# Two of four late modulation products moved from VectorE to GpSimd, their loads from ScalarE's queue to SyncE's

## What is computed

```
def _layer(x, c, positions, norm_g, w_ada, b_ada, w_in, ...):
    mod = jax.nn.silu(c) @ w_ada + b_ada
    shift, scale, gate = jnp.split(mod, 3, axis=-1)
    h = _rmsnorm(x, norm_g) * (1.0 + scale[:, None, :]) + shift[:, None, :]
    proj = h @ w_in
    ...
    xbc = jax.nn.silu(_causal_dwconv(xbc, conv_w, conv_b))
    ...
    y = _ssd(xs, dt, A, Bm, Cm) + d_skip[:, None] * xs      # uses cumulated sums of dt * A
    ...
    out = mixed @ w_out
    return x + gate[:, None, :] * out
```

## Time and profile before

| | |
|---|---|
| median of three executions | 3406.31 us |
| the profiled execution, its own time | 3412.05 us |
| its span in the trace | 3410.0 us |
| mean granted TensorE clock | 0.984 |
| PE busy | 3296.2 us, 97% |
| DVE busy | 1748.1 us, 51% |
| ACT busy | 1191.9 us, 35% |
| POOL busy | 410.4 us, 12% |

### The profile page before, as it was taken

How to read it: one execution, slowest core, us unless ns; L and a number is a source line. 1 busy time by engine, 2 the same in 40 slices (tenths; PEclk the granted TensorE clock), 3 DMA queues, 4 the chain that set the end, 5 groups by cost and what they waited for, 6 DMA issues and landing times.

```text
span 3410.0 us, 44406 instructions
## 1 busy us (share of the span) xinstructions
PE 3296.2 (97%) x18526; PEld 2620.8 (77%) x18526; DVE 1748.1 (51%) x2533; ACT 1191.9 (35%) x1884; POOL 410.4 (12%) x318
## 2 busy tenths in 40 slices
PE   6999999899999999999999999999999999999999
PEld 5776777686677888887777778888888887678887
DVE  6854455644446743336767654433565334454333
ACT  3334442434443432224333342222343224332221
POOL 0000010000001311002222211100101011011110
PEclk9899999899999999999989999999999999899999
DMA  5631122221122333224200013322323323012332
GB/s 218 201 124 56 56 99 83 78 87 62 56 77 73 105 105 99 97 88 128 69 20 3 19 46 121 99 94 89 103 86 99 97 89 93 10 64 94 99 98 81
DMA packets 83911, 295.47 MB, mean 87 GB/s; under 512 B 9472, under 2 KB 12800, under 8 KB 81664
## 3 DMA queue, kind: packets, MB, share of 16 engines
q1 hardware_dynamic: 78384, 270.61, 24.5%
q10 hardware_dynamic: 5328, 22.02, 2.0%
HBM read 283.94 MB, written 8.65 MB: 86 GB/s over the span
## 4 chain that ended last, share of the span: by engine, by line
PE 83%; DVE 7%; ACT 2%; issue 2%; POOL 1%; DMA 1%; DVEq 0%; ACTq 0%; POOLq 0%
PE acc L478 66%; PE acc L1508 1%; DVE w_lo L389 1%; DMA late_ada<-in_ada 1%; PE acc L2487 1%; PE acc L3261 1%; PE aux L3225 1%; PE aux L1789 1%; ACT w_hi L382 1%; PE acc L1820 1%; DVE ssd_ex L1410 1%; PE acc L2491 1%; PE acc L2477 1%; PE aux L2444 1%; PE aux L3230 1%
## 5 line engine op out<-in xcount | busy, mean ns | idle before, releaser
L478 PE MATMUL acc<-op_hi,w_hi 128*128 128x512 f32 x2624 | 1086.6, 414 | 25.7 <-ACT conv_sums L1201 11.8
L478 PE MATMUL acc<-op_hi,w_lo 128*128 128x512 f32 x2624 | 1030.5, 393 | 0.0
L478 PE MATMUL acc<-op_lo,w_hi 128*128 128x512 f32 x2624 | 1029.3, 392 | 0.0
L382 ACT ACTIVATE w_hi<-raw 128x1024 fp32r<-128x1024 f32 (+2 forms) x476 | 494.4, 1039 | 1529.4 <-PE acc L478 1499.5
L389 DVE TENSOR_TENSOR w_lo<-raw,w_hi 128x1024 fp32r<-128x1024 f32 (+2 forms) x476 | 577.0, 1212 | 291.9 <-ACT w_hi L382 291.6
L478 PEld LDWEIGHTS acc<-op_hi,w_hi 128*128 128x128 f32 x2624 | 496.5, 189 | 186.0 <-issue 83.9
L478 PEld LDWEIGHTS acc<-op_hi,w_lo 128*128 128x128 f32 x2624 | 495.9, 189 | 107.5
L478 PEld LDWEIGHTS acc<-op_lo,w_hi 128*128 128x128 f32 x2624 | 497.6, 190 | 102.9 <-issue 10.1
L478 PE MATMUL acc<-ffn_hi,w_hi 128*128 128x512 f32 x800 | 311.5, 389 | 0.0
L478 PE MATMUL acc<-ffn_hi,w_lo 128*128 128x512 f32 x800 | 311.3, 389 | 0.0
L478 PE MATMUL acc<-ffn_lo,w_hi 128*128 128x512 f32 x800 | 311.3, 389 | 0.0
(11 more groups left out here) (583 smaller groups left out, 3889.3 us busy)
## 6 DMA issues: line engine op xcount, KB each, us to landing
raw<-in_w SPq DMA_DIRECT2D x436, 512.0 KB, 3.5
late_ada<-in_ada ACTq DMA_DIRECT2D x32, 512.0 KB, 4.2
raw<-in_w SPq DMA_DIRECT2D x32, 384.0 KB, 3.0
ada<-in_ada ACTq DMA_DIRECT2D x4, 1024.0 KB, 14.3
ada<-in_ada SPq DMA_DIRECT2D x4, 1024.0 KB, 21.7
x_mid<-x SPq DMA_DIRECT2D x16, 256.0 KB, 3.3
x<-x_mid SPq DMA_DIRECT2D x2, 2048.0 KB, 8.6
skew<-rel_rows SPq DMA_DIRECT2D x12, 192.0 KB, 2.8
```

The source lines that it names most:

```text
L382: act.activation(self.w_hi[g % AHEAD][:, 0:k, :], self.raw[s][:, 0:k, :], ACT.Copy).then_inc(self.split_hi.handle, 1)
L478: mm = pe.matmul(self.bank(s, g), w[:, k, :], a[:, k, 0:s.n], start=(k == 0 and q == 0), stop=(k == k_tiles - 1 and q == 2))
```

## The change

It has five parts.

1. `later` keeps two jobs, (0, 2) and (1, 0), on DVE, with a row each 5.3 of planned time. A second `Modulation`, `beside`, does (1, 1) and (1, 2) with the same start and pace. Its 16 rows run on POOL, with two slots (`beside_ada`) and a sum (`beside_sum`) of its own.
2. POOL has the two steps of a row in two instructions: TENSOR_SCALAR multiplies the slot in place, TENSOR_TENSOR adds it to the sum. A job's first row needs only the first.
3. All 32 loads are issued by SP, between its loads of weight pieces, in place of ACT.
4. PE's column sums come in two pairs in place of four singles, with one bank for each `Modulation`.
5. POOL clears `self.cum` and writes the row of ones, in place of DVE, and DVE waits for both before its scans.

```
 class Startup(Stage):
-            dve.memset(core.ones_row[:, :], 1.0).then_inc(*self.rows.inc())
+    def pool(self, pool):
+        def ones():
+            yield 0.0
+            pool.memset(self.core.ones_row[:, :], 1.0).then_inc(*self.rows.inc())
 class Modulation(Stage):
...
+    def pool(self, pool):
         def rows():
-            m, core = len(self.slots), self.core
+            m, core, out = len(self.slots), self.core, self.sums[0]
             for c in range(self.chunks):
                 yield self.start + c * self.pace
-                job, part = divmod(c, self.parts)
-                out = self.sums[job % len(self.sums)]
+                job, k = divmod(c, KD)
+                row = self.slots[c % m][:, 0, :]
                 if c == 0:
...
+                    pool.wait_ge(*self.cond)
+                pool.wait_ge(*self.landed[c % m].ge(16 * (c // m + 1)))
+                if k == 0:
+                    if job:
+                        pool.wait_ge(*self.summed.ge(job))
+                    pool.tensor_scalar(out, row, core.cond[:, 0:1], None, ALU.mult).then_inc(*self.stepped.inc())
+                    continue
+                pool.tensor_scalar(row, row, core.cond[:, k:k + 1], None, ALU.mult).then_inc(*self.scaled.inc())
+                pool.wait_ge(*self.stepped.ge(c))
+                pool.wait_ge(*self.scaled.ge(job * (KD - 1) + k))
+                pool.tensor_tensor(out, out, row, ALU.add).then_inc(*self.stepped.inc())
+        return (rows(),) if self.on_pool else ()
...
-            step(dve.memset(self.cum, 0.0))
...
+            dve.wait_ge(*self.cum_zeroed.ge(1))
+            dve.wait_ge(*self.ones_made)
...
+        def zeros():
+            yield self.t0 - 6.0
+            for count in self.cum_free:
+                pool.wait_ge(*count)
+            pool.memset(self.cum, 0.0).then_inc(*self.cum_zeroed.inc())
...
-    later = Modulation(core, [(0, 2), (1, 0), (1, 1), (1, 2)], 1, ada("late_ada", 1, (-52, 72)),
-                       [core.ss_pair[:, :, :].rearrange("p i t -> p (i t)")], startup.cond.ge(1), at=0.0, pace=2.65,
-                       issuer=lambda c: "act")
+    later = Modulation(core, [(0, 2), (1, 0)], 1, ada("late_ada", 1, (-52, 72)),
+                       [core.ss_pair[:, :, :].rearrange("p i t -> p (i t)")], startup.cond.ge(1), at=0.0, pace=5.3,
+                       issuer=lambda c: "sp", banks=core.acc[2:3])
+    beside = Modulation(core, [(1, 1), (1, 2)], 1, ada("beside_ada", 1, (56, 60)), [core.beside_sum[:, :]],
+                        startup.cond.ge(1), at=0.0, pace=5.3, issuer=lambda c: "sp", name="ada_beside",
+                        banks=core.acc[3:4], on_pool=True)
...
-    later.start = linear.starts[1] + 20.0
+    later.start = beside.start = linear.starts[1] + 20.0
```

More of the change, by code:

```diff
@@ L1034, in __init__ @@
         self.chunks = chunks
-        self.landed = [core.share(f"ada_landed{i}", 16 * len(range(i, chunks, m))) for i in range(m)]
-        self.stepped = core.share("ada_step", n * KD)
-        self.summed, self.made = core.share("ada_summed", n), core.share("ada_made", 2 * n)
+        self.landed = [core.share(f"{name}_landed{i}", 16 * len(range(i, chunks, m))) for i in range(m)]
+        self.stepped = core.share(name + "_step", n * KD)
+        self.scaled = core.share(name + "_scaled", n * (KD - 1) if on_pool else 0)
+        self.summed, self.made = core.share(name + "_summed", n), core.share(name + "_made", 2 * n)
     def load(self, eng, c):
@@ L1063, in act, with rows_on @@
         return (self.loads(("act", act)),)
-    def dve(self, dve):
+    def rows_on(self, eng):
+        m, core = len(self.slots), self.core
+        for c in range(self.chunks):
+            yield self.start + c * self.pace
+            job, part = divmod(c, self.parts)
+            out = self.sums[job % len(self.sums)]
+            if c == 0:
+                eng.wait_ge(*self.cond)
+            if part == 0 and job >= len(self.sums):
+                eng.wait_ge(*self.summed.ge(job - len(self.sums) + 1))
+            eng.wait_ge(*self.landed[c % m].ge(16 * (c // m + 1)))
+            for i in range(self.rows):
+                k = part * self.rows + i
+                if k == 0:
+                    ins = eng.tensor_scalar(out, self.slots[c % m][:, i, :], core.cond[:, 0:1], None, ALU.mult)
+                else:
+                    eng.wait_ge(*self.stepped.ge(job * KD + k))
+                    ins = eng.scalar_tensor_tensor(out=out, in0=self.slots[c % m][:, i, :],
+                                                   scalar=core.cond[:, k:k + 1], in1=out, op0=ALU.mult, op1=ALU.add)
+                ins.then_inc(*self.stepped.inc())
@@ L1103, in biased @@
                     dve.sem_inc(*self.made.inc())
-        return rows(), biased()
+        return (biased(),) if self.on_pool else (self.rows_on(dve), biased())
     def pe(self, pe):
@@ L3897, in program @@
     linear = Linear(core, segments, at=25.0)
[L3899 to L3902 removed]
+    later.start = beside.start = linear.starts[1] + 20.0
+    layers[0].ssd.cum_free, layers[1].ssd.cum_free = [now.stepped.ge(2 * KD)], [layers[0].of_others.lo.ge(KC)]
+    layers[0].ssd.ones_made = layers[1].ssd.ones_made = startup.rows.ge(1)
+    layers[0].ssd.after, layers[0].ssd.banks_free = [rstd0.made.ge(1)], [later.ready(), beside.ready()]
+    layers[0].ssd.sums_free = startup.angles_free = [later.ready()]
+    later.free, beside.free = [norm0.src.ge(KD)], [now.stepped.ge(2 * KD)]
+    layers[0].fox.slots_free.append(beside.stepped.ge(2 * KD))
     layers[0].gate_free.append(later.stepped.ge(len(later.jobs) * KD))
     layers[0].times(linear, 0)
[L3905 to L3906 removed]
+    startup.angles_at = later.start + 17 * later.pace + 4.0
+    layers[0].before[0:0] = [later.ready(), beside.ready()]
     begin = linear.starts[second] - 14.0
```

49 lines of the change are left out of this document (19 added, 30 removed).

## The result

The change makes the kernel slower. Beside each other on one chip the median is 3426.97 us after and 3406.64 us before, thirteen executions each. The ratio is 1.0049, with an interval of 1.004 to 1.0059. It is taken over all executions and is not the quotient of the two medians (that would be 1.006). A second set of the same two kernels gave 1.0043 (1.0026 to 1.006).

A forecast was written before the change was run, and what follows sets the result against it. PE was taken as the bound, with DVE just ahead. Terms +2.6 + 6.8 - 2.0 - 1.95 - 1.35 + 1.95 + 1.0 make +7.05 us on the 3406.3 us median, about 3413.5; range 3400 to 3432.

The forecast's parts named there:

- PE is the bound and waits for banks that DVE's chain frees: Convolution tiles: PE is busy, DVE just ahead; a chain slower by over 0.3 us a tile shows on PE.
- exclusive turns of DVE and POOL: Where both read SBUF, the engines take turns; a POOL pair costs DVE about 3.5 us.
- The price of POOL's instructions: POOL's rows of 1024: sum 2.4 us, product about 1.5 us, so a pair 3.9 us.
- (a): Up to the release of tile 4: net +2.6 us, bounds -2.2 and +4; PE's wait before tile 6 is 9 to 10.
- (b): The seven releases from tile 4 to tile 11: 8.6 us a tile against 7.65, +6.8 us.
- (c): At tile 13, PE's slack is used up first: -2.0 us, so that tile starts 7.4 us late.
- (e): End of the jobs: POOL ends at 198.2 us; PE's last wait 1.0 us, before 2.35 (-1.35); a two-job column group, +1.95.
- POOL becomes the last: Rival, chance 0.15: product 2.4 us, not 1.5; 6.3 us in (b), 7 in (e), 5 showing; about +19 us, 3425.
- (f): More short waits of PE mean more half clock, mostly inside time DVE takes anyway: +1.0 us.
- rare collisions: Rival, chance 0.10: POOL slips into DVE's waits and PSUM work; tile 4's bank 2.2 us earlier; -4.5 us, 3402.
- the early bank: Rival, chance 0.10: the wait before tile 6 and the low clock behind it go; up to -13.9 us, 3392.

The follow-up runs named there:

- e4: Changed kernel with POOL's product and sum of 14 of its 16 rows cut to one column of 1024; 0.9990 of the kernel before.
- e3: Changed kernel with the 16 rows of `beside` back on DVE, all else kept; 1.0000 of the kernel before.
- e5: Changed kernel with POOL's sums cut to one column, its products whole; 1.0004 of the kernel before.
- e7: Changed kernel with one job, (1, 2), on POOL and three on DVE, paces 10.6 and 3.53; 1.0029 of the kernel before.
- e1: The changed kernel once more, unedited; 3429.08 us against 3412.48 for the kernel before, ratio 1.0043.
- e9: Changed kernel with all four jobs on DVE as one sequence, four slots, rows only behind DVE's scans (start 28.0, not 20.0); 0.9978 of the kernel before.
- e6: Changed kernel with POOL's products cut to one column, its sums whole; 1.0017 of the kernel before.

## Why the prediction was right, and where its sizes were off

It said slower by 7 us as the likeliest (3413.5), with a range of 3400 to 3432. Measured were 3426.97 in one set (16.7 us over before by its ratio) and, by the ratio of the other, some 14.6 us. So the side and the range held, and the size foretold was half of what was measured. The chances were less sure than the forecast: slower by over 0.2% had 0.46 (its own terms, 0.30 and 0.15, make 0.45).

- **PE is the bound and waits for banks that DVE's chain frees.** Right. The added waits are for L1229, `ssd_ncum` and `w_lo`, all on DVE's chain.
- **The mechanism, exclusive turns of DVE and POOL.** Shown: with POOL's work on one column, or on DVE, the loss is gone (e4, e3). The Trainium skill, SBUF — State Buffer, section "Who interferes with whom", says that the loser blocks for the whole instruction. For the sums the trace agrees (DVE's row stood from 104.65 until POOL's end at 106.97). For the products the traces do not: DVE lost 0.5 us per product of 2.85 us or more, and e5 is 1.3 us over e4 at the mark.
- **The price of POOL's instructions.** The sum was priced at 2.4 us and takes 2.34. The product was priced at 1.5 us, from a COPY, and takes 2.85: the upper bound of 2.4 was below it too. The Trainium skill, GPSIMD Engine Reference, section 4.1, calls one-input work roughly line-rate; here DVE does the same TENSOR_SCALAR in 0.75 us. The measurement decides.
- **(a) Tile 4: +2.6 us.** Wrong in size: -0.2 us in one execution of the changed kernel, and +2.0 in the other, where 1.8 us of it are older. ACT's wait went as said. PE's wait is 7.7 us, not the 9 to 10 that was to show it. In e7, where the first row and pair fall on the same instructions, the bank does come 4.2 us late: the step was possible, and depended on where the data land. In the changed kernel the collisions ahead of tile 4 cost DVE 3.2 us (two L389 of 1.97 and 2.85 us for 1.22, three L1244 of 3.16 for 2.32), where 4.8 were put in.
- **(b) Seven releases at 8.6 us: +6.8 us.** Measured 8.5 us each, and 9.0 in the second execution (62.8 / 7). But the number is right by errors that cancel, which is luck. A pair cost DVE 2.2 us, not 3.5, which is 9.3 us less over seven. Against that, one row more stayed on DVE (1.2 us). The work that was there before was read 1.75 us too low: DVE was busy for 48.45 of the 53.53 us, not 46.7, since 1.7 of the 2.2 us of idle time at L1216 in the earlier trace rows lie ahead of 101.88. The copies of 3.8 us that were to lie beside POOL for nothing hid nothing that shows. And DVE was idle for 3.7 us (55.95 busy of 59.65), not 2.0, most of it for ACT's `w_hi` (2.9 us), which stands behind the silu that waits for DVE.
- **(c) Slack of 2.0 us.** The size came out and the path did not. At tile 13 PE is 7.4 us late, as the sum said (L1513 at 169.24 us answers to L1477 at 161.81 before), and the column sums begin at 199.71; the sum said 199.8. But the bank of tile 11 is only 5.9 us late, and PE does not wait for it. The last bank that it waits for is the one of tile 9, at 146.68 us (140.60 before), and from there it runs at its own pace, with half clock behind the wait and behind the column sums.
- **(e) The end of the jobs.** The wait was to be 1.0 us and under 3, and is 2.19 in both executions. POOL's second job began at 155.59 us (154 was said) and lasted to 203.69, not to 198.2, because a first row and each product are dearer than said. To this extent *POOL becomes the last* happened; its other half, 6.3 us more in (b), did not, since the product hardly blocks DVE.
- **(f) More half clock: +1.0 us.** This is the term that was too small. Up to the mark the changed kernel is 8.6 and 14.0 us late, against 7.05 foretold, and over whole executions it is 15 to 17 us by the ratios. Two of the new waits have a stretch at 0.50 at them (the granted clock between 105.5 and 160.2 us is 0.87, and 0.98 from 110.9 to 194.4 in the earlier trace rows). In e1's set the clock accounts for an estimated 4 us, and at equal clock some 10 are left. How the lower mean clock divides between the stretch of the change and the rest of an execution, no run separates.

The rival *POOL becomes the last* had 3425, nearer to the measured 3426.97 than the forecast, and its condition, a product of 2.4 us or more, came true. Its path did not: (b) did not grow by 6.3 us, and the last wait is 2.19 us. That its number is near is luck.

Of the other rivals, rare collisions is out (all seven of POOL's sums from 97.69 to 145.25 us met a DVE instruction that got longer), and the early bank did not come in the changed kernel. In e9 it comes 4.3 us earlier (3.2 counted from tile 0), and with the last wait gone as well the mark is 10.5 us ahead.

## What to carry to other kernels

Work that is moved to an idle engine is free only if the two engines don't make each other stand still, as these two do: add to its own time what it makes the other stand still, instruction by instruction, and compare that with what is taken away (here 2.2 us for 1.2). Where the bound engine waits once for a long time, look first at what stands ahead of the release of its bank, and at loads that are asked for just when they are needed; starting the same rows 8 us later, with slots to load ahead, brought the mark further ahead (200.35 us) than POOL's rows made nearly free (206.98 in e4). A trace of one execution locates a loss; where the clock differs from one execution to the next by more than the loss, only sets of executions size it.

## What the runs showed of the hardware that was not expected

- On GpSimd a TENSOR_SCALAR of 128x1024 in float32, in place, takes 2.85 us undisturbed, longer than a TENSOR_TENSOR of that size (2.34 us). Beside DVE it takes up to 4.88.
- Of the two, the longer one disturbs VectorE less: about 0.5 us each (e5) against 1.6 us (e6). Both get longer beside VectorE's instructions: in the changed kernel's convolution tiles the product more (mean 3.50 us for 2.85) than the sum (2.44 for 2.34), but each by itself about alike (3.20 in e5, 2.83 in e6). What makes the difference inside the engine wasn't tried.
- Where a collision falls counts: with half the pairs the mark is at 219.21 us (e7), as in one of the two traces with all of them (219.44 and 224.84), and 3.7 us of its collisions fell on the path ahead of a wait.
